# A two-part residual network kernel with fifteen own buffers for the first modulation's weights, and the pooled stage computed after its product

## The chip, the cores and the metric

The kernel runs on one core of a Trainium2 chip. The metric is device microseconds of one execution; before the change the three timed runs took 959.43, 956.2 and 955.88 us, median 956.2 us.

## The reference, cut to what matters

x is 256 tokens by 1024 features, all in fp32. The first of two stacks has two layers of two sublayers, each `x = x + gate * f(rms_norm(x) * (1 + scale) + shift)`. Shift, scale and gate come from one vector c: `silu(c) @ ada_w[layer, sub] + ada_b`, a 1024 x 3072 product for a single row, four times over (12 MB of weights each). f is, in turn: a hybrid of gated linear attention and sliding-window attention; an MLP (1024 to 4096, relu squared, back to 1024); the pooled mixer; and the same MLP with other weights. The second stack has an attention and retention mixer, a gated convolution MLP and an embedding gate.

The pooled mixer is the one that the change turns around:

```python
for gi, w in enumerate((2, 4, 8, 16)):          # 256 features per group
    csg = cs[..., lo:hi]                         # cumulative sums over tokens
    lag = jnp.pad(csg, ((0, 0), (w, 0), (0, 0)))[:, :S]
    pooled = (csg - lag) / cnt - hf[..., lo:hi]  # cnt = min(t + 1, w)
    outs.append(pooled.astype(h.dtype) @ pool_w[gi])
return jnp.concatenate(outs, axis=-1) * pool_scale
```

## The kernel before, in words

**Layout.** X lives in SBUF feature-major, eight tiles X[:, t, :] of 128 features by 256 tokens. Every fp32 operand of a large product is split into a high part rounded to fp32r and a low part, and a product is three fp32r matmuls (hi*hi, hi*lo, lo*hi: L557 to L559).

**Weight blocks.** All weights but the modulation's go through 135 numbered blocks of 1 MB (eight tiles of 128 x 256). Block n is loaded by SyncE into raw[n % 4] once w_lo of block n - 4 is made (L408), ScalarE makes w_hi (`split_hi`, L1786), VectorE makes w_lo (`split_lo`, L1123), and TensorE uses them (`block_used`). w_hi and w_lo have two buffers each, so the split of block n + 2 begins when block n is used. The order of work on each engine is written out by hand; each engine's program is one straight list with semaphores, so an instruction that waits holds everything behind it.

**Modulation.** The 96 pieces of ada_w (128 x 1024, 512 KB) are loaded by GpSimd, and VectorE multiplies each by one value of silu(c) per partition and adds it to an accumulator (`ada_sum`, L1142; first ones L1137). Pieces 0 to 7 are the first sublayer's scale, 8 to 15 its shift, 16 to 23 its gate. They go through three slots ada_raw, except `ADA_EARLY`, which have places of their own: six halves of the raw buffers and two attention tiles. The sum over the 128 partitions is then taken either by TensorE transposes into a PSUM bank and a VectorE reduction (`turn_sums` L660, `part` L1174), or by 1-column matmuls with ones (`add_sums`, L670; the second sublayer's gate and the third's three parts).

**Opening.** SyncE issues constants, c, x, thirteen small vectors, rel_bias, w_gla, sinks and the 16 glr columns; then `t8` (the relative bias table, a matmul L743) goes to DRAM (L435) and comes back skewed (`hankel`, tile MIX, L439, after 10 sums), and TensorE flips it (L758, four 128 x 512 fp32 products) between the scale's turn and the shift's turn (L660). Then `norm` (L1285), ScalarE's high part with the shift (L1808), VectorE's low part (L1268), and block 0.

**Attention.** The first sublayer's gate is turned between blocks 2 and 3. After the attention, ScalarE makes the mix's high part (L1813), then `split_hi(10)`; VectorE the low part (L1265), then `split_lo(10)`.

**MLP.** `up`: 16 blocks; VectorE fits 2, 1, 2, 1 sums of ada pieces into the four blocks of an iteration. `down`: four iterations of four blocks into PSUM A[0] and A[1], one iteration for two tiles of X; VectorE has 2, 2, 0, 0 sums after the splits, then `residual_tile` for both tiles (L1246, L1250, L1256), a split, and 2 more sums.

**Pooled stage.** After `down(0)`: scale sums (L670), the mean square of x (L649, root on ScalarE L1792, L1795), VectorE makes `factor(2)` and writes h without shift to pad[0] (L1560), waits for the shift sums (L670, `part` L1167), ScalarE adds the shift (L2030), VectorE runs 1 to 4 shifted additions per group (L1576), divides (L1583, L1584, L1587), ScalarE and VectorE split (L2035, L1265), and TensorE multiplies with block 45. The residual (L1215) needs the gate's sum. ScalarE squares X (L2040), TensorE sums (L941), and the last sublayer's norm (L1285, L1808, L1268) leads to `up(1)`.

## Time and profile before

| | |
|---|---|
| runs timed | 955.88, 956.2, 959.43 us; median 956.2 |
| profiled execution, its own time | 958.09 us |
| its span, first to last instruction | 956.4 us |
| TensorE busy, mean granted clock | 888.4 us (93%), 0.97 |
| VectorE busy | 692.1 us (72%) |
| ScalarE busy | 456.8 us (48%) |
| DMA | 196.60 MB, mean 206 GB/s |

### The profile page before, as it was taken

How to read it: one execution, taken by the hardware profiler on the slowest of the kernel's cores; microseconds unless marked ns; L12 is line 12 of the kernel's file. 1: busy time of each engine (PE TensorE's matmuls, PEld its weight loads, DVE VectorE, ACT ScalarE, POOL GpSimd, SP SyncE). 2: the span in 40 equal slices, each digit the busy share in tenths (PEclk: the TensorE clock that was granted, in tenths of full speed). 3: DMA queues.
4: the chain of work that ended last, by engine and by line, in shares of the span. 5: the costliest groups of instructions: out<-in, count | busy, mean ns of one | idle time of the engine just before them, and what ended most of it. 6: DMA issues, size and time to landing. Idle time of an engine off the chain costs nothing.

```text
span 956.4 us, 17671 instructions
## 1 busy us (share of the span) xinstructions
PE 888.4 (93%) x7028; PEld 852.6 (89%) x7028; DVE 692.1 (72%) x877; ACT 456.8 (48%) x573; POOL 58.0 (6%) x104
## 2 busy tenths in 40 slices
PE   2599999899999996799999999999999999999996
PEld 1388879799999996699999999988989999999996
DVE  4889878788878888766666556855487877776665
ACT  2347464566643333456663433444465444444445
POOL 2110110211111110000000000000000000000000
PEclk9789999999999996799999999999999999999998
DMA  9895755499989994057765555653435555654531
GB/s 336 300 339 193 244 200 177 130 319 322 317 306 330 330 316 134 23 184 234 239 199 176 175 183 168 197 166 130 157 90 177 177 179 187 218 173 158 169 126 44
DMA packets 156600, 196.60 MB, mean 206 GB/s; under 512 B 5341, under 2 KB 143116, under 8 KB 156556
## 3 DMA queue, kind: packets, MB, share of 16 engines
q1 hardware_dynamic: 142732, 145.64, 47.6%
q0 software_dynamic: 13824, 50.34, 14.4%
q8 instruction: 31, 0.51, 0.2%
q14 instruction: 13, 0.11, 0.0%
HBM read 194.90 MB, written 1.06 MB: 205 GB/s over the span
## 4 chain that ended last, share of the span: by engine, by line
PE 81%; DVE 9%; ACT 4%; issue 2%; DMA 2%; SPq 1%; DVEq 0%; ACTq 0%
PE G L557 15%; PE G L558 15%; PE G L559 15%; PE A L557 7%; PE A L559 7%; PE A L558 7%; DVE w_lo L1123 2%; ACT w_hi L1786 2%; PE G L632 2%; PE A L685 2%; PE G L633 2%; PE G L634 2%; DMA sinks<-in_attn_sinks_dram 1%; DMA MIX<-bias_rows 1%; DVE HN L1285 1%
## 5 line engine op out<-in xcount | busy, mean ns | idle before, releaser
L1123 DVE TENSOR_TENSOR w_lo<-raw,w_hi 128x2048 fp32r<-128x2048 f32 x135 | 307.1, 2275 | 163.7 <-ACT w_hi L1786 163.5
L1786 ACT ACTIVATE w_hi<-raw 128x2048 fp32r<-128x2048 f32 x135 | 256.6, 1901 | 265.7 <-PE A L559 132.4
L557 PE MATMUL G<-h_hi,w_hi 128*128 128x256 f32 x880 | 257.9, 293 | 22.5 <-DVE h_lo L1268 13.0
L558 PE MATMUL G<-h_lo,w_hi 128*128 128x256 f32 x880 | 253.3, 288 | 0.0
L559 PE MATMUL G<-h_hi,w_lo 128*128 128x256 f32 x880 | 253.2, 288 | 0.0
L557 PEld LDWEIGHTS G<-h_hi,w_hi 128*128 128x128 f32 x880 | 173.0, 197 | 29.5 <-issue 22.5
L558 PEld LDWEIGHTS G<-h_lo,w_hi 128*128 128x128 f32 x880 | 173.6, 197 | 0.2 <-issue 0.2
L559 PEld LDWEIGHTS G<-h_hi,w_lo 128*128 128x128 f32 x880 | 173.2, 197 | 0.0
L557 PE MATMUL A<-u_hi,w_hi 128*128 128x256 f32 x512 | 143.4, 280 | 0.7 <-DVE w_lo L1123 0.7
L558 PE MATMUL A<-u_lo,w_hi 128*128 128x256 f32 x512 | 142.9, 279 | 0.0
L559 PE MATMUL A<-u_hi,w_lo 128*128 128x256 f32 x512 | 142.9, 279 | 0.0
L557 PE MATMUL G<-e_hi,w_hi 128*128 128x256 f32 x368 | 104.2, 283 | 0.0
L558 PE MATMUL G<-e_lo,w_hi 128*128 128x256 f32 x368 | 104.2, 283 | 0.0
L559 PE MATMUL G<-e_hi,w_lo 128*128 128x256 f32 x368 | 104.1, 283 | 0.0
L557 PEld LDWEIGHTS A<-u_hi,w_hi 128*128 128x128 f32 x512 | 96.2, 188 | 1.3 <-DVE w_lo L1123 1.3
L558 PEld LDWEIGHTS A<-u_lo,w_hi 128*128 128x128 f32 x512 | 96.2, 188 | 0.0
L559 PEld LDWEIGHTS A<-u_hi,w_lo 128*128 128x128 f32 x512 | 96.2, 188 | 0.0
L557 PEld LDWEIGHTS G<-e_hi,w_hi 128*128 128x128 f32 x368 | 70.7, 192 | 0.0
L558 PEld LDWEIGHTS G<-e_lo,w_hi 128*128 128x128 f32 x368 | 70.7, 192 | 0.0
L559 PEld LDWEIGHTS G<-e_hi,w_lo 128*128 128x128 f32 x368 | 70.7, 192 | 0.0
L1142 DVE SCALAR_TENSOR_TENSOR ada_acc<-ada_raw,c_silu,ada_acc 128x1024 f32<-128x1024 f32 x52 | 65.7, 1280 | 4.7 <-DMA ada_raw<-in_ada_w_dram 3.7
L557 PE MATMUL A<-f_hi,w_hi 128*128 128x256 f32 x176 | 49.7, 282 | 1.8 <-DVE HN L1240 1.8
(325 smaller groups left out, 1315.7 us busy)
## 6 DMA issues: line engine op xcount, KB each, us to landing
raw<-in_mlp_w_dram SPq DMA_DIRECT2D x64, 1024.0 KB, 5.5
ada_raw<-in_ada_w_dram POOLq DMA_DIRECT2D x88, 512.0 KB, 5.7
raw<-in_w_in_dram SPq DMA_DIRECT2D x14, 1024.0 KB, 5.0
raw<-in_w_up_dram SPq DMA_DIRECT2D x11, 1024.0 KB, 5.4
raw<-in_w_gate_dram SPq DMA_DIRECT2D x11, 1024.0 KB, 5.3
raw<-in_attn_w_in_dram SPq DMA_DIRECT2D x9, 1024.0 KB, 7.1
raw<-in_w_down_dram SPq DMA_DIRECT2D x8, 1024.0 KB, 5.2
raw<-in_attn_w_out_dram SPq DMA_DIRECT2D x4, 1024.0 KB, 5.4
```

What stands on the lines that cost most here:

```text
L557: pe.matmul(dst, wh, ah, start=start, stop=False)
L558: pe.matmul(dst, wh, al, start=False, stop=False)
L559: return pe.matmul(dst, wl, ah, start=False, stop=stop)
L632: pe.matmul(dst, h_hi[:, t, toks], w_hi[n % 2][:, t, cols], start=t == 0, stop=False)
L633: pe.matmul(dst, h_hi[:, t, toks], w_lo[n % 2][:, t, cols], start=False, stop=False)
L634: last = pe.matmul(dst, h_lo[:, t, toks], w_hi[n % 2][:, t, cols], start=False, stop=t == KT - 1)
L685: last = pe.matmul(dst[:, e, 0:keys], Q4[half, hp, b * P:b * P + P], K4[half, kt, 0:keys], start=True, stop=True)
L1123: dve.tensor_tensor(w_lo[n % 2][:, 0:k, :], raw[n % RAW][:, 0:k, :], w_hi[n % 2][:, 0:k, :].bitcast(F32), ALU.subtract).then_inc(lo_done, 1)
L1142: dve.scalar_tensor_tensor(out=acc, in0=src, scalar=c_silu[:, bass.ds(i * 2 + k, 1)], in1=acc, op0=ALU.mult, op1=ALU.add).then_inc(ada_use ...
L1285: ins = dve.scalar_tensor_tensor(out=HN[p % 2][:, m, :], in0=X[:, t, :], scalar=gain[:, t:t + 1], in1=roots[:, :], op0=ALU.mult, op1=ALU.mult)
L1786: act.activation(w_hi[n % 2][:, 0:k, :], raw[n % RAW][:, 0:k, :], ACT.Copy).then_inc(hi_done, 1)
```

## The change

**Opening.** Pieces 3 to 15 and 19, 20 now have places of their own (five raw halves and ten tiles that the attention needs only later), so scale and shift are issued without waiting, but for piece 15, which waits for the table's way to DRAM; gate pieces wait for raw block 1. rel_bias is loaded third and its table is sent before x; x is issued behind the thirteen vectors. The skewed table is fetched before block 0, not after ten sums. The scale is summed along rows by ScalarE (`rows_along`, four copies in place with accumulator reads); VectorE norms the four pairs into HN0 with pieces 11 to 14 between them, then splits block 0, then adds piece 15; the shift's two halves are summed by ScalarE and VectorE, and only the two splits with the shift follow. The first gate is turned after the attention and summed by ScalarE before `split_hi(10)`.

**Pooled stage.** The product comes first: X times the gain, split like e_hi and e_lo inside `down(0)`, is multiplied with block 45 token-major; the result is scaled with the token's root and the shift's own product (sw, made by two ones matmuls from parts made in `down(0)`) is added, and the pooling is four 128 x 144 and 128 x 128 band matrices, applied by fp32 matmuls. VectorE makes the bands in `down(0)`. The sums of the second sublayer's gate and the third's scale and shift are turned between `up(0)` and `down(0)` in the G banks; up's sums stand as 2, 2, 2, 0; the last iteration of down has its last two before the residual. Three blocks of up(1) are loaded before SyncE waits for the sw parts.

```diff
-ADA_EARLY = (3, 4, 5, 6, 7, 8, 19, 20)
+ADA_EARLY = (*range(3, 16), 19, 20)
...
-                 for n in range(6)] + [b[:, :, :].rearrange("p t s -> p (t s)") for b in (GE, GG)]
+                 for n in range(5)]
+        early += [b[:, :, :].rearrange("p t s -> p (t s)") for b in (Q4, K4, V4, GV)] + [
+            PT[:, :, :, :].rearrange("p a b s -> p (a b s)"),
+            wide[:, 4:6, :].rearrange("p a b -> p (a b)"), wide[:, 6:8, :].rearrange("p a b -> p (a b)"),
+            SS[:, :, :, :].rearrange("p a b s -> p (a b s)")]
...
-                sp.dma_start(x_rows, x[0].rearrange("(k p) d -> p k d", p=P)).then_inc(x_in, 16)
+                sp.dma_start(rb[:, :], rel_bias).then_inc(rb_in, 16)
...
+                bank_was_read(sp, "table")
+                sp.dma_start(scratch.ap(), t8[:, :]).then_inc(table_out, 16)
+                sp.dma_start(x_rows, x[0].rearrange("(k p) d -> p k d", p=P)).then_inc(x_in, 16)
...
                 sp.wait_ge(table_out, 16)
-                sp.wait_ge(ada_used, 10)
                 sp.dma_start(hankel[:, :, :],
                              bass.AP(scratch, 0, [[1, P], [HANKEL, HEADS], [1, S]])).then_inc(table_in, 16)
+                load(N_ATTN, w_in[:, :, ATTN_COLS[0]:ATTN_COLS[0] + COLS])
+                sp.wait_ge(early_full[ADA_EARLY.index(2 * DT - 2)], 16)
                 for j, col in enumerate(ATTN_COLS[1:], 1):
                     if j < RAW:
-                        sp.wait_ge(ada_used, (14, 16, 16)[j - 1])
+                        sp.wait_ge(ada_used, (5, 7, 8)[j - 1])
...
+                if f == 2 * DT - 1:
+                    pool.wait_ge(table_out, 16)
+                if f == 2 * DT:
+                    pool.wait_ge(raw_full[1], 16)
...
-            def add_sums(m, name, blocks):
...
+            def turned_free(m, part, u, blocks):
                 pe.wait_ge(ada_used, blocks)
-                for t in range(DT):
-                    last = pe.matmul(dst[:, t:t + 1], sums_of(m, part)[:, part, t * P:(t + 1) * P],
-                                     ones[:, 0:1], start=True, stop=True)
-                bank_done(f"{name}{m}", last)
-            def scale_and_shift(m):
-                for name in ("scale", "shift"):
-                    turn_sums(m, name, {1: ADA_C, 3: ADA_E}[m])
+                for half in range(2):
+                    g_empty(u + half)
+                    for t in range(4):
+                        at = (4 * half + t) * P
+                        last = pe.transpose(G[(u + half) % 4][:, t * P:(t + 1) * P],
+                                            sums_of(m, part)[:, part, at:at + P], ident)
+                    last.then_inc(sums_turned, 1)
+            def token_sums(name, norm):
+                pe.wait_ge(ssq_ready, SQUARES[norm])
...
-            turn_sums(0, "gate", ADA_B)
...
+            turn_sums(0, "gate", ADA_B)
...
-            add_sums(1, "gate", ADA_D - 2)
+            for n, (m, part) in enumerate(((1, GATE), (2, SCALE), (2, SHIFT))):
+                turned_free(m, part, U_SUMS + 2 * n, ADA_D)
             down(0)
-            add_sums(2, "scale", ADA_D)
-            mean_square(2)
-            add_sums(2, "shift", ADA_D)
-            add_sums(2, "gate", ADA_E)
             block_ready(N_POOL)
+            def pool_group(g):
+                pe.wait_ge(e2_ready, 2 * g + 2)
+                for k in range(2):
+                    u = U_POOL + 2 * (g // 2) + k
+                    if g % 2 == 0:
+                        g_empty(u)
+                    dst = halves(G[u % 4])[:, g % 2, :]
+                    toks = slice(k * P, k * P + P)
+                    for t in (2 * g, 2 * g + 1):
+                        pe.matmul(dst, h_hi[:, t, toks], w_hi[N_POOL % 2][:, t, :], start=t == 2 * g, stop=False)
+                        pe.matmul(dst, h_hi[:, t, toks], w_lo[N_POOL % 2][:, t, :], start=False, stop=False)
+                        last = pe.matmul(dst, h_lo[:, t, toks], w_hi[N_POOL % 2][:, t, :], start=False,
+                                         stop=t % 2 == 1)
+                return last
+            pool_group(0)
+            pool_group(1).then_inc(pool_done, 1)
+            pool_group(2)
+            token_sums("ms2", 2)
+            pe.wait_ge(sw_ready, 1)
+            for p in range(2):
+                pe.wait_ge((down_free0, down_free1)[p], 5)
+                dst = bank_empty(pe, f"sw{p}")
+                bank_done(f"sw{p}", pe.matmul(halves(dst), ones[:, :], HN[p][:, :, :], start=True, stop=True))
+            turn_sums(2, "gate", ADA_E)
+            pool_group(3).then_inc(block_used, 1)
+            turn_sums(3, "scale", ADA_E)
             for g in range(4):
-                g_empty(U_POOL + g)
+                if g == 2:
+                    turn_sums(3, "shift", ADA_E)
+                for k in range(2):
+                    u = U_POOL + 2 * (g // 2) + k
+                    pe.wait_ge(g_free[u % 4], u // 4 + 1)
+                u = U_POOL + 4 + g
+                g_empty(u)
                 for m in range(2):
-                    if m == 0:
-                        pe.wait_ge(h_ready, 4 * SPLIT["pool"] + g + 1)
-                    last = feature_tile(N_POOL, halves(G[(U_POOL + g) % 4])[:, m, :], slice(m * P, m * P + P),
-                                        [(2 * g, 2 * g), (2 * g + 1, 2 * g + 1)], h_hi, h_lo)
-                last.then_inc(pool_done if g < 3 else block_used, 1)
-            scale_and_shift(3)
+                    dst = halves(G[u % 4])[:, m, :]
+                    cols = slice(g * COLS + m * P, g * COLS + m * P + P)
+                    pe.matmul(dst[:, 0:P + POOL_PAD], z_tok[:, 0, cols], band[:, g, :], start=True, stop=False,
+                              skip_group_check=True)
+                    last = pe.matmul(dst[:, P:S], z_tok[:, 1, cols], band2[g], start=False, stop=True,
+                                     skip_group_check=True)
+                last.then_inc(band_done, 1)
...
+            ada_next(6)
...
+            for p in range(4):
+                for t in (2 * p, 2 * p + 1):
+                    ins = dve.scalar_tensor_tensor(out=HN0[:, t, :], in0=X[:, t, :], scalar=GAIN[:, 0, t:t + 1],
+                                                   in1=rstd[:, :], op0=ALU.mult, op1=ALU.mult)
+                ins.then_inc(norm_ready, 1)
+                ada_next(1)
...
-                        for _ in range((2, 1, 2, 1)[j] if with_ada else 0):
+                        for _ in range((2, 2, 2, 0)[j] if with_ada else 0):
...
-                    part(1, "gate")
+                    for half in range(2):
+                        u = U_SUMS + half
+                        dve.wait_ge(sums_turned, half + 1)
+                        ins = dve.tensor_reduce(part_sums[:, 4 * half:4 * half + 4],
+                                                G[u % 4][:, :].rearrange("p (t k) -> p t k", t=4), AX_X, ALU.add)
+                        ins.then_inc(g_free[u % 4], 1)
+                        dve.wait_ge(g_free[u % 4], u // 4 + 1)
...
+                    for u in range(U_SUMS + 2, U_SUMS + 6):
+                        dve.wait_ge(g_free[u % 4], u // 4 + 1)
+                    chain(with_bias(6 * DT, 2 * DT, 0))
+                    chain(factor(2))
...
+                def band_of(g):
+                    v, head = C[:, C_DIST:C_DIST + P + POOL_PAD], band[:, g, 0:POOL_PAD]
+                    chain(dve.tensor_scalar(band[:, g, :], v, -float(P), 1.0 / (2 << g), ALU.is_ge, ALU.mult))
+                    chain(dve.scalar_tensor_tensor(out=band[:, g, :], in0=v, scalar=float((2 << g) - P),
+                                                   in1=band[:, g, :], op0=ALU.is_lt, op1=ALU.mult))
+                    chain(dve.tensor_tensor(band2[g], band[:, g, 0:P], ident, ALU.subtract))
+                    chain(dve.scalar_tensor_tensor(
+                        out=head, in0=v[:, 0:POOL_PAD], scalar=-float(P),
+                        in1=C[:, C_CNT_AT + g * POOL_PAD:C_CNT_AT + (g + 1) * POOL_PAD],
+                        op0=ALU.is_ge, op1=ALU.mult))
+                    chain(dve.scalar_tensor_tensor(out=head, in0=v[:, 0:POOL_PAD], scalar=float((2 << g) - P),
+                                                   in1=head, op0=ALU.is_lt, op1=ALU.mult))
+                    dve.tensor_tensor(band[:, g, 0:P], band[:, g, 0:P], ident, ALU.subtract)
+                def out_tiles(i, last, bands=()):
...
+                        if j == 2:
+                            for g in bands:
+                                band_of(g)
+                        if j == 2 and last:
+                            dve.wait_ge(sw_part, 1)
+                            for g in range(4):
+                                part = HN[g // 2][:, g % 2, :]
+                                at = 2 * g + 1
+                                ins = dve.scalar_tensor_tensor(out=part, in0=raw[N_POOL % RAW][:, at, :],
+                                                               scalar=MOD[:, 2, at:at + 1], in1=part,
+                                                               op0=ALU.mult, op1=ALU.add)
+                            ins.then_inc(sw_ready, 1)
+                        for _ in range((2, 2, 2 if last else 0, 0)[j] if with_ada else 0):
...
+                if layer == 0:
+                    for i, bands in enumerate(((0,), (1,), (2, 3), ())):
+                        out_tiles(i, i == 3, bands)
...
+            for p in range(2):
+                if p == 0:
+                    dve.wait_ge(pool_done, 1)
+                else:
+                    dve.wait_ge(block_used, N_POOL + 1)
+                bank_was_read(dve, f"sw{p}")
+                for k in range(2):
+                    u = U_POOL + 2 * p + k
+                    dve.scalar_tensor_tensor(out=z_tok[:, k, 512 * p:512 * p + 512], in0=G[u % 4][:, :],
+                                             scalar=t_rstd[:, k:k + 1], in1=sw[:, p, :], op0=ALU.mult,
+                                             op1=ALU.add).then_inc(g_free[u % 4], 1)
+            for half in "ab":
+                bank_was_read(dve, f"gate2{half}")
+            chain(with_bias(8 * DT, DT, 0))
             chain(dve.tensor_tensor(gate_ps[:, :], MOD[:, 2, 2 * DT:], V[:, V_PSCALE:V_PSCALE + DT], ALU.mult))
             for g in range(4):
...
+            def rows_along(bank, col):
+                for t in range(4):
+                    tile = bank[:, t * P:(t + 1) * P]
+                    ins = act.activation(tile, tile, ACT.Copy,
+                                         accum_out=mod_sums[:, col + t:col + t + 1])
+                return ins
...
+            for half in range(2):
+                src = bank_full(act, f"gate0{'ab'[half]}")
+                bank_read(f"gate0{'ab'[half]}", rows_along(src, 2 * DT + 4 * half))
             split_hi(10)
...
+            token_root("ms2", t_rstd)
+            for p in range(2):
+                src = bank_full(act, f"sw{p}")
+                bank_read(f"sw{p}", act.activation(sw[:, p, :], src[:, :], ACT.Copy))
+            for name, col in (("gate2", 0), ("scale3", 2 * DT), ("shift3", DT)):
+                for half in range(2):
+                    src = bank_full(act, f"{name}{'ab'[half]}")
+                    bank_read(f"{name}{'ab'[half]}", rows_along(src, col + 4 * half))
```

## Rows read from the trace of the kernel before

**Rows 1.** Windows over the span's stages

```profile
core 0: us, PE busy (x) PEld busy (x) DVE busy (x) ACT busy (x) POOL busy (x), PEclk, DMA share, GB/s
0.00:48.40 48.40, 17.88 (x62) 11.97 (x62) 30.91 (x45) 13.96 (x23) 11.34 (x25) 0.89 0.89 319
...
361.50:401.30 39.80, 25.46 (x135) 23.55 (x133) 32.69 (x72) 13.85 (x25) 1.42 (x2) 0.69 0.22 68
```

**Rows 2.** Windows of the opening, the same columns

```profile
12.00:20.00 8.00, 2.05 (x10) 1.43 (x8) 5.04 (x5) 2.06 (x4) 1.06 (x2) 1.00 1.03 384
...
28.00:36.00 8.00, 0.83 (x8) 0.59 (x6) 7.69 (x10) 2.69 (x3) 1.58 (x3) 0.76 0.81 263
```

**Rows 3.** DMA issues to 60 us: x, KB each, median us to landing

```profile
wide<-in_x_dram SPq DMA_DIRECT2D x1, 1024.0 KB, 9.6
MIX<-bias_rows SPq DMA_DIRECT2D x1, 1024.0 KB, 8.6
```

**Rows 4.** Timeline of all engines to 75 us: start, duration, what, idle before

```profile
18.89 0.71 PE L739 MATMUL A<-C,PR 128*128 128x128 f32 x3 [5.56 <-DMA PR<-in_conv_w_dram]
...
21.65 1.97 PE L729 MATMUL A<-C,wide 128*128 128x128 f32 x8
...
36.91 6.38 PE L758 MATMUL A<-MIX,C 128*128 128x512 f32 x8 [8.08 <-DMA MIX<-bias_rows]
...
48.44 0.36 PE L557 MATMUL G<-h_hi,w_hi 128*128 128x256 f32 x1 [4.27 <-DVE h_lo L1268]
```

**Rows 5.** Timeline of TensorE: end of block 0 (next product)

```profile
58.02 0.28 PE L557 MATMUL A<-h_hi,g_hi 128*16 128x256 f32 x1
```

**Rows 6.** Timeline of TensorE: turn of the first gate

```profile
76.23 1.04 PE L660 MATMUL A<-C,ada_acc 128*128 128x128 f32 x8
```

**Rows 7.** Groups by line: count, busy, mean ns (VectorE)

```profile
L1123 DVE TENSOR_TENSOR w_lo<-raw,w_hi 128x2048 fp32r<-128x2048 f32 x131 | 300.0, 2290 | 157.1 <-ACT w_hi L1786 156.9
L1142 DVE SCALAR_TENSOR_TENSOR ada_acc<-ada_raw,c_silu,ada_acc 128x1024 f32<-128x1024 f32 x52 | 65.7, 1280 | 4.7 <-DMA ada_raw<-in_ada_w_dram 3.7
...
L1174 DVE TENSOR_REDUCE part_sums<-A 128x4 f32<-128x512 f32 x16 | 11.0, 688 | 2.2 <-PE A L660 1.9
```

**Rows 8.** Groups by line: ScalarE's split, accumulator read, PSUM copy

```profile
L1786 ACT ACTIVATE w_hi<-raw 128x2048 fp32r<-128x2048 f32 x131 | 250.7, 1913 | 256.8 <-PE G L559 129.9 <-PE A L559 123.4 <-DMA raw<-in_attn_w_in_dram 2.5
...
L1841 ACT ACTIVATION_READ_ACCUMULATOR PR<-SS,stat 128x1 f32 x32 | 6.1, 189 | 0.0
...
L1848 ACT ACTIVATE MIX<-A 128x128 f32<-128x128 f32 x8 | 2.2, 272 | 1.2 <-PE A L707 1.2
```

**Rows 9.** VectorE: the low part of block 10

```profile
147.06 2.29 DVE L1123 TENSOR_TENSOR w_lo<-raw,w_hi 128x2048 fp32r<-128x2048 f32 x1 [1.11 <-ACT w_hi L1786]
```

**Rows 10.** TensorE between up(0) and down(0)

```profile
270.00 1.92 PE L670 MATMUL A<-ones,ada_acc 128*128 128x1 f32 x16
```

**Rows 11.** VectorE in the last block of up(0)

```profile
275.52 0.68 DVE L1513 TENSOR_TENSOR u_lo<-HN,u_hi 128x512 f32 x1
```

**Rows 12.** VectorE in down(0), third iteration: waits for ScalarE's split

```profile
324.43 2.29 DVE L1123 TENSOR_TENSOR w_lo<-raw,w_hi 128x2048 fp32r<-128x2048 f32 x1 [0.92 <-ACT w_hi L1786]
...
341.22 2.29 DVE L1123 TENSOR_TENSOR w_lo<-raw,w_hi 128x2048 fp32r<-128x2048 f32 x1 [0.39 <-ACT w_hi L1786]
```

**Rows 13.** TensorE around the pooled stage

```profile
361.47 1.84 PE L670 MATMUL A<-ones,ada_acc 128*128 128x1 f32 x16
...
395.33 1.89 PE L941 MATMUL A<-HN,ones 128*128 128x256 f32 x8
401.30 0.55 PE L557 MATMUL G<-h_hi,w_hi 128*128 128x256 f32 x1 [4.07 <-DVE h_lo L1268]
```

**Rows 14.** TensorE's granted clock around short stands (columns as rows 1)

```profile
139.00:145.00 6.00, 3.24 (x27) 2.27 (x25) 4.38 (x7) 4.20 (x10) 0.00 (x0) 1.00 0.02 9
...
366.00:390.00 24.00, 15.29 (x68) 14.70 (x69) 20.86 (x48) 6.49 (x13) 1.42 (x2) 0.51 0.14 45
401.00:408.00 7.00, 6.64 (x29) 6.09 (x30) 5.82 (x12) 3.62 (x5) 0.00 (x0) 0.53 0.01 2
```

302 lines of the change are left out of this document (160 added, 142 removed).

## The prediction

> **What bounds the kernel now.** I read the windows of the stages first [rows 1]. In the first 48.4 us TensorE is busy for 17.9 us, and in the 39.8 us from the end of `down(0)` to the first product of `up(1)` for 25.5 us at a mean clock of 0.69. In between it is nearly always busy, and there a change of another engine matters only if it makes TensorE wait. So the chain of waits was read in these two stretches, and the timelines of VectorE and ScalarE wherever the change gives them work beside TensorE.
>
> In the opening the reader is to see three things. The 16 DMA engines move 384 GB/s at first but only 263 GB/s at 28 to 36 us [rows 2]: pieces queue behind sums. VectorE and TensorE wait for the thirteen vectors, which are turned at 18.9 us. And the flips of the skewed table stand at 36.9 to 43.1 us, ahead of the shift's turn [rows 4]. Block 0 starts at 48.44 and ends at 58.0 [rows 4, 5].
>
> In the pooled stage VectorE is busy 32.7 of 39.8 us [rows 1], and TensorE stands at the lower clock, 0.51 from 366 to 390 us [rows 14].
>
> **Part 1, the opening.** Scale and shift are 16 pieces of 0.52 MB; with x, the table, block 0's weights and constants about 12 MB, at 384 GB/s [rows 2] 31 us. DMA ends near 33 us, so VectorE's list decides. x is now issued at about 9.5 us; with its 9.6 us of before [rows 3] it lands at 19 (bounds: 14, if it was the queue ahead of it that was slow, and 27, if the whole backlog goes first). Four turns, and ScalarE's square and copy of each pair, 1.1 us, end at 24; mean square, scale turn (eight transposes took 1.97 us on a TensorE that had stood [rows 4], 1.04 on a running one [rows 6]) and root at 26. `rows_along` is a PSUM copy and an accumulator read, 272 and 189 ns [rows 8], some 0.3 us with overlap: eight are 2.4 us, GAIN at 28.4. VectorE has by then done eleven sums; the vectors, no longer behind x, should reach it at about 15. Then four pairs of HN0 (0.85 each) with four sums at 1.2 (1280 ns, overlapped [rows 7]): 36.6; split of block 0 2.2 [rows 7] and g_lo: 39.1; last sum 40.3; turn at the lower clock 42.2; reduction 0.69 [rows 7] and two small sums 43.1; high part 44.1, low part 45.0. Block 0 starts 3.4 us earlier. Pairs then come every 0.9 us instead of every 1.65, and block 0, half of it at the lower clock, ends at 53.7: **-4.3 us**. Between -8 (x at 14) and +1 (x at 27, less what shorter waits at the end return).
>
> **Part 2, the first gate.** Its turn among the attention's products goes: -1.0 us [rows 6]. On ScalarE eight copies now stand before `split_hi(10)`. Before, the low part of block 10 waited 1.1 us for ScalarE and ended at 149.3 [rows 9], just before TensorE needed it. Plus 2.4 us it ends at 151.7; with some 0.6 us of lead TensorE waits 1.8. VectorE's two reductions are gone, in cover. Together **+0.8** (0 to +2).
>
> **Part 3, between up(0) and down(0).** Before, this seam cost TensorE 1.8 us [rows 10]. Now 24 transposes go into G banks, and the bank of the fifth turn is the first one's, that of the sixth the second's. They come free only by VectorE's reductions, which stand behind its last u_lo. That began at 275.5 after a sum of 1.2 us that is no longer there [rows 11]; so it ends at about 275.1, the reductions at 275.8 and 276.5, and the turns at 277.0. `down(0)` starts 5.2 us later than at 271.8 [rows 10]. ScalarE's own sixteen copies end at 278.6, before its next split is due. In these 7 us TensorE does 3 us of transposes. After a stand of 4.07 us [rows 13] it ran at 0.53 over 401 to 408 us [rows 14], 3 us lost; in 139 to 145 us, half busy, it kept 1.00 [rows 14]. I take 1.0. **+6.2** (+3 to +9).
>
> Here a rule speaks against the change. The trace shows the stretch of 139 to 145 us, which holds products and turns mixed, at the full clock [rows 14]. The Trainium skill ("TensorE: Matmul & The Clock Gate", Part 4: PE-mode transpose) says that transposes do not count as busy for the clock. By it this seam and the turns in the pooled stage would fall to 1.2 GHz; no row isolates this. It is the fourth case below.
>
> **Part 4, down(0).** VectorE gets 0.95 us of low parts per iteration and the bands. Two rows give it about 0.27 us plus 1 ns an element (1280 ns at 1024, 2290 at 2048 [rows 7]); with overlap 0.3 for 144 elements, 0.2 for 16: 1.6 us a band. What VectorE has over is 0.92 us at most blocks and 0.39 after the residual [rows 12], and of a block's 5.6 us ScalarE's split (1.9 [rows 8]) and VectorE's (2.3 [rows 7]), which begin when the buffer is free, leave some 1.3 us of lead. One band: 1.6 + 0.95 - 0.6 - 1.3 = 0.65 us of wait at the first block of the next iteration and 0.4 at its second, twice; two bands: 2.25 and 0.4. **+4.7** (+1, if the leads add up, to +7). The up loop's 2, 2, 2, 0 is hidden: its one-sum blocks had more over than a sum costs.
>
> **Part 5, the pooled stage**, counted from the end of `down(0)`. In the last iteration VectorE still has the split of block 45, the sw parts (1.9) and two sums (2.4) when TensorE is through: squares are ready at +5.5, e2's last low part at +6.5, the split of 46 at +9.3. TensorE: groups 0 to 2, 36 products at 0.117 us (16 blocks of 48 took the 89.6 us from 271.9 to 361.5 [rows 10, 13]): +4.2; waits for the squares +5.5; token sums +6.0; sw +7.9 (a 256-column fp32 product is 0.47 us [rows 13], 512 columns twice that); gate turn +8.9; group 3 +10.3; scale turn +11.3; bands 0, 1 +13.1; shift turn +14.1; bands 2, 3 +15.9. VectorE's z are ready before them; the residual ends at +16.9. ScalarE has 24 accumulating copies, 0.3 each, and comes to the squares of X late: +18.4. Sum +19.0, and from there root, norm and split as before, 4.1 us (397.2 to 401.3 [rows 13]): +23.05, against 39.8 [rows 1]. **-16.8** (-20 to -9, the latter if TensorE stays at the lower clock for half of it).
>
> Blocks from `up(1)` on are as before: the three blocks loaded early, and SyncE's wait for sw_ready behind them, are 15 us ahead of use. GpSimd's waits for the table and for raw block 1 hold only the gate's pieces, wanted after 50 us.
>
> **Sum**: -4.3 + 0.8 + 6.2 + 4.7 - 16.8 = -9.4 us. The profiled execution took 958.09 us for a span of 956.4 and would take 948.7; the median of the runs, 956.2, lies 1.9 below it, so the median after is 946.8, say **947**.
>
> **Rivals.**
> 1. The forecast, 942 to 951: 0.46.
> 2. The leads hold: VectorE's lateness in `down(0)` is absorbed (part 4 near +1, and squares then 2 us earlier), x lands early. For it: VectorE waited for ScalarE's splits before [rows 12], so there is time to catch up. Against: its new work stands in lumps. 956.2 - 9.4 - 5.7 = 941: 0.20.
> 3. The opening returns nothing: x lands at 27 us behind the thirteen pieces, and everything from the scale's root shifts. For it: in the first 20 us the engines are full [rows 2]. Against: x had its landing within 9.6 us with nine pieces queued [rows 3]. +4.3: 951: 0.14.
> 4. The lower clock holds at the seam (+2) and through half the pooled stage's turns and bands (+6): 955: 0.13.
> 5. Slower: the same mechanism through the whole stage. The seam costs 3 us more and its transposes 2; of the work from +6.0 to +15.9 all 9.9 us double, and the last sums and the opening's turns add 1.5: +16, 963 us. It decides from the point where TensorE is at 0.5 for over 14 us of work that I priced at full speed. For it: 24 us at 0.51 in this very place before [rows 14]. Against: TensorE comes to it from 90 us at the full clock and stands only 1.3 us. 0.07.
>
> **How the numbers follow.** A measurement of this kernel tells 0.5%, 4.8 us, from no change; the bound is 951.4. Faster: cases 1 and 2 and nearly half of 3: 0.72. Same: the rest of 3, case 4: 0.21. Slower: case 5: 0.07. The range leaves out case 5 and the tail of case 2 and takes in the others: 939 to 955.5. The cases of both signs are not close, so it is one range.
>
> **What would show it.** In the changed profile: first product of block 0 near 45 us, with the last sum's turn just ahead; one TensorE wait before block 10; a gap of 6 to 7 us between the last product of `up(0)` and the first of `down(0)` with two VectorE reductions in it; waits for w_lo in the iterations after the bands; 23 us from `down(0)` to `up(1)`, at a clock near 1. The prediction is wrong in part 1 if x lands before 15 or after 25 us, in part 3 if the clock after the seam is 0.5 for a block, in part 4 if the waits for w_lo are under 2 us, and as a whole if these stages balance.

## The result, and the profile after

The changed kernel takes 966.75 us (median of 4 runs, 964.47 to 967.42) against 957.57 us (4 runs, 955.88 to 959.43) for the kernel before: ratio 1.009, 95% interval 1.0066 to 1.0114. It is slower by 0.9%; I had said 947 and faster. The profiled execution took 964.47 us for a span of 962.8, so the forecast of -9.4 us stands against +6.4 between the two traces. The medians lie 9.2 us apart: the traced execution was 2.3 us under its kernel's median, that of the kernel before 0.5 above. The ledger below explains the 6.4.

Windows of the changed kernel over its stages, the columns of [rows 1]:

```profile
core 0: us, PE busy (x) PEld busy (x) DVE busy (x) ACT busy (x) POOL busy (x), PEclk, DMA share, GB/s
0.00:52.06 52.06, 17.43 (x63) 11.71 (x63) 30.63 (x47) 17.69 (x49) 11.38 (x25) 0.85 1.00 360
52.06:60.10 8.04, 8.04 (x49) 8.02 (x50) 7.00 (x10) 3.03 (x5) 0.00 (x0) 0.70 0.30 89
...
274.70:281.50 6.80, 3.15 (x26) 2.57 (x25) 6.09 (x7) 6.34 (x23) 1.05 (x2) 1.00 1.01 348
281.50:382.00 100.50, 93.92 (x771) 92.90 (x770) 77.49 (x90) 35.01 (x39) 11.08 (x21) 0.98 0.77 264
382.00:406.70 24.70, 18.77 (x133) 16.63 (x132) 17.79 (x36) 15.90 (x65) 1.42 (x2) 0.97 0.36 110
406.70:962.80 556.10, 543.75 (x4416) 530.33 (x4416) 369.51 (x470) 269.39 (x303) 3.69 (x7) 0.99 0.52 168
```

TensorE sets the end in every stage, so the first and last products of the stages make a ledger that closes:

| stage | before | after | measured | forecast |
|---|---|---|---|---|
| start to end of block 0 (part 1) | 58.02 | 60.03 | +2.0 | -4.3 |
| from there to up(0) (part 2) | 117.34 | 119.93 | +2.6 | +0.8 |
| up(0) | 94.56 | 94.61 | 0.0 | 0 |
| seam (part 3) | 1.86 | 6.90 | +5.0 | +6.2 |
| down(0) (part 4) | 89.70 | 100.46 | +10.8 | +4.7 |
| pooled stage (part 5) | 39.82 | 24.81 | -15.0 | -16.8 |
| up(1) to the end | 555.1 | 556.1 | +1.0 | 0 |
| sum | 956.4 | 962.8 | +6.4 | -9.4 |

The turned pooled stage gives its 15 us, at a granted clock of 0.97 against 0.69 [rows 1]. Four other stages spend more than that. Two rows of the table hold most of the miss: the opening (6.3 us) and down(0) (6.1 us).

**The opening.** The timeline of the changed kernel, all engines. x turns at 19.99 and the norm is multiplied from 30.49 on, about as forecast. But then:

```profile
34.64 6.29 PE L798 MATMUL A<-MIX,C 128*128 128x512 f32 x8 [7.00 <-DMA MIX<-bias_rows]
...
41.46 1.90 ACT L1912 ACTIVATE w_hi<-raw 128x2048 fp32r<-128x2048 f32 x1
...
43.39 2.29 DVE L1194 TENSOR_TENSOR w_lo<-raw,w_hi 128x2048 fp32r<-128x2048 f32 x1 [4.86 <-ACT w_hi L1912]
...
45.80 1.28 DVE L1213 SCALAR_TENSOR_TENSOR ada_acc<-SS,c_silu,ada_acc 128x1024 f32<-128x1024 f32 x1
...
47.22 1.94 PE L695 MATMUL A<-C,ada_acc 128*128 128x128 f32 x8 [6.30 <-DVE ada_acc L1213]
...
52.06 0.55 PE L592 MATMUL G<-h_hi,w_hi 128*128 128x256 f32 x1 [2.90 <-DVE h_lo L1339]
```

Read it from below: the first product waits for the shift, the shift's turn for the sixteenth sum, that sum stands behind block 0's low part, the low part behind its high part, the high part on ScalarE behind the four copies of the flips, and the flips wait for the skewed table. The table's row among the DMA issues says how late it was (8.6 us before [rows 3]):

```profile
wide<-in_x_dram SPq DMA_DIRECT2D x1, 1024.0 KB, 10.8
MIX<-bias_rows SPq DMA_DIRECT2D x1, 1024.0 KB, 19.8
```

**down(0).** Who TensorE waits for from 281.5 to 388 us:

```profile
PE A L592 <- DVE X L1317: 6.1, 3, 3.0
PE A L716 <- DVE sq_sum L1327: 1.2, 1, 1.2
PE A L592 <- DVE w_lo L1194: 0.4, 2, 0.2
```

and VectorE, in the same stretch:

```profile
DVE w_lo L1194 <- ACT w_hi L1912: 11.3, 8, 5.5
DVE late_acc L1213 <- DMA ada_raw<-in_ada_w_dram: 8.5, 7, 2.7
```

I had expected TensorE to wait for low parts. It waits 0.4 us for those and 6.1 us for `X`: the residual that reads banks A[0] and A[1] and so frees them. There is one pair of them, so the next output pair can't begin before. The worst of the three, as both engines show it:

```profile
350.65 1.28 DVE L1213 SCALAR_TENSOR_TENSOR late_acc<-ada_raw,c_silu,late_acc 128x1024 f32<-128x1024 f32 x1 [1.57 <-DMA ada_raw<-in_ada_w_dram]
351.86 2.28 DVE L1194 TENSOR_TENSOR w_lo<-raw,w_hi 128x2048 fp32r<-128x2048 f32 x1
354.06 0.23 DVE L1634 TENSOR_SCALAR band<-C 128x144 f32<-128x144 f32 x1
...
357.17 0.48 DVE L1317 SCALAR_TENSOR_TENSOR X<-A,MOD,X 128x256 f32<-128x256 f32 x1
...
357.70 0.58 PE L592 MATMUL A<-u_hi,w_hi 128*128 128x256 f32 x1 [3.04 <-DVE X L1317]
```

A sum that waits 1.57 us for its piece, a split, two bands (3.1 us) and only then the residual. Behind this stand TensorE's products come 0.21 us apart instead of 0.12 until 360.8: 1.4 us more. The products before and after it come at another pace than before the change too; that is the last group of experiments.

### The profile page after: what moved, and what is told of

The parts are those of the page before. It is cut to its first block, busy times and chain, and to the rows that moved or that the text cites. A ratio compares the mean times of both kernels' runs of the same rounds, so it can differ in the third digit from the quotient of the medians.

```text
span 962.8 us, 17732 instructions
## 1 busy us (share of the span) xinstructions
PE 888.2 (92%) x7036; PEld 850.9 (88%) x7036; DVE 682.9 (71%) x872; ACT 472.8 (49%) x695; POOL 58.0 (6%) x104
## 4 chain that ended last, share of the span: by engine, by line
PE 75%; DVE 10%; ACT 5%; DMA 5%; issue 3%; SPq 1%; ACTq 0%; DVEq 0%; POOLq 0%
PE G L592 14%; PE G L593 14%; PE G L594 14%; PE A L592 6%; PE A L594 6%; PE A L593 6%; DVE w_lo L1194 3%; ACT w_hi L1912 2%; DMA ada_raw<-in_ada_w_dram 2%; DMA MIX<-bias_rows 2%; PE G L667 2%; PE G L668 2%; PE G L669 2%; PE A L727 2%; DVE late_acc L1213 1%
## 5 line engine op out<-in xcount | busy, mean ns | idle before, releaser
L592 PE MATMUL G<-h_hi,w_hi 128*128 128x256 f32 x864 | 250.8, 290 | 15.2 <-DVE h_lo L1339 11.2
L593 PE MATMUL G<-h_lo,w_hi 128*128 128x256 f32 x864 | 246.8, 286 | 0.0
L594 PE MATMUL G<-h_hi,w_lo 128*128 128x256 f32 x864 | 246.6, 285 | 0.0
L592 PEld LDWEIGHTS G<-h_hi,w_hi 128*128 128x128 f32 x864 | 167.9, 194 | 21.2 <-issue 14.3
L593 PEld LDWEIGHTS G<-h_lo,w_hi 128*128 128x128 f32 x864 | 168.3, 195 | 0.2 <-issue 0.2
L594 PEld LDWEIGHTS G<-h_hi,w_lo 128*128 128x128 f32 x864 | 168.1, 195 | 0.0
L592 PE MATMUL A<-u_hi,w_hi 128*128 128x256 f32 x512 | 145.8, 285 | 6.6 <-DVE X L1317 6.1
L1213 DVE SCALAR_TENSOR_TENSOR ada_acc<-ada_raw,c_silu,ada_acc 128x1024 f32<-128x1024 f32 x45 | 57.1, 1280 | 5.4 <-DMA ada_raw<-in_ada_w_dram 4.9
```

The lines of the kernel that those rows point to most:

```text
L592: pe.matmul(dst, wh, ah, start=start, stop=False)
L593: pe.matmul(dst, wh, al, start=False, stop=False)
L594: return pe.matmul(dst, wl, ah, start=False, stop=stop)
L1213: dve.scalar_tensor_tensor(out=acc, in0=src, scalar=c_silu[:, bass.ds(i * 2 + k, 1)], in1=acc, op0=ALU.mult, op1=ALU.add).then_inc(ada_use ...
```

## The experiments

Medians, and ratios to the kernel before on the same chip. The runs were made on several chips, so where two variants are compared closely the ratios and their intervals count, not the difference of the medians.

| run | base and edit | us | ratio (95%) |
|---|---|---|---|
| e1_split_first | after, opening's order | 963.22 | 1.0076 (1.0055 to 1.0097) |
| e2_hold | e1, seven pieces held for the table | 962.85 | 1.0055 (1.0026 to 1.0083) |
| e7_hold_x | e1, five pieces held for x | 961.05 | 1.0028 (1.0005 to 1.0050) |
| e10_opening2 | after, x early, shift's turn first | 962.72 | 1.0036 (1.0009 to 1.0062) |
| h1_opening_only | before, with after's opening | 963.75 | 1.0049 (1.0031 to 1.0067) |
| h3_opening_ordered | h1, with e1's order | 959.12 | 1.0001 (0.9990 to 1.0013) |
| e4_bands_seam | after, bands ahead of down(0) | 960.71 | 1.0030 (1.0019 to 1.0040) |
| e5_bands_after | after, bands behind the sums | 960.23 | 1.0030 (1.0017 to 1.0043) |
| e8_last | e4, residual first at the end | 956.96 | 0.9999 (0.9986 to 1.0011) |
| e3_seam_gate | after, six banks; block 10 first | 961.33 | 1.0039 (1.0026 to 1.0053) |
| c2_all | all of it | 949.85 | 0.9905 (0.9869 to 0.9942) |
| c3_all | e10's opening, bands 3 + 1 | 947.15 | 0.9875 (0.9848 to 0.9902) |
| c4_all | c3 with e1's opening | 946.06 | 0.9852 (0.9826 to 0.9877) |
| p1_spare96 | before, one unused tile | 960.88 | 1.0028 (1.0013 to 1.0043) |
| p2_mod256 | c4, u and f moved back | 944.49 | 0.9850 (0.9830 to 0.9870) |
| p3_h32 | p2, h moved by 32 bytes | 938.63 | 0.9795 (0.9772 to 0.9817) |
| p5_e32 | p3, e moved too | 933.83 | 0.9756 (0.9734 to 0.9778) |
| p4_before_h32 | before, h moved by 32 bytes | 952.62 | 0.9945 (0.9925 to 0.9966) |

### The opening

**e1_split_first.**

```diff
@@ ScalarE
+            split_hi(0)
             for q in range(4):
                 src = bank_full(act, f"flip{q}")
...
-            split_hi(0)
@@ VectorE
+            ada_next(1)
             split_lo(0)
...
-            ada_next(1)
```

> The changed kernel with two moves in the opening and nothing else: ScalarE splits block 0 ahead of the four copies of the flips, and VectorE does the sixteenth sum ahead of block 0's low part. Theory (order): the changed kernel's block 0 starts at 52.06 us because the high part (41.5 to 43.4) stood behind copies that wait for the skewed table, and the last sum and the shift's turn stood behind the low part. Block 0's weights are in by about 37.6 us, so high part to 39.5, low part to 42, sum by 40, turn 41 to 43 behind the last flip, first product at 46.5: 5.5 us earlier, about 961 against 966.75. Rival (the loads decide): block 0's own weights or the piece land so late that the order is worth under 1.5 us, about 966.

The timeline of this kernel, the same places as above:

```profile
35.90 1.91 ACT L1912 ACTIVATE w_hi<-raw 128x2048 fp32r<-128x2048 f32 x1 [5.07 <-DMA raw<-in_attn_w_in_dram]
...
37.59 1.28 DVE L1213 SCALAR_TENSOR_TENSOR ada_acc<-SS,c_silu,ada_acc 128x1024 f32<-128x1024 f32 x1
...
44.04 0.36 PE L592 MATMUL G<-h_hi,w_hi 128*128 128x256 f32 x1 [3.61 <-DVE h_lo L1339]
```

The first product stands 8.0 us earlier than in the trace of the changed kernel, and no load was issued otherwise. But not all of the 8.0 is order: the table landed at 32.8 us here and at 34.6 there. In the six traces with the changed kernel's opening (after, e3, e4, e5, e8, h1) the first product stands at 49.8 to 52.1, in the six with this order (e1, h3, c4, p2, p3, p5) at 44.0 to 45.5, so order is worth about 6 us. The theory holds for the place. In the medians 3.5 us are left, and the intervals of the two ratios overlap. Part of that is block 0's clock: in this trace it ran at full speed, 6.0 us long, in the eight others with the two moves (e2, e7, h3, c2, c4, p2, p3, p5) partly or mostly at the lower clock, 7.0 to 8.5; and the traced execution (958.13) was by 4.4 us the fastest of the five. In it down(0), with its stops, took 103.5 us, 3.1 more than in the changed kernel.

**e2_hold** and **e7_hold_x.**

```diff
@@ GpSimd, e2
-                if f == 2 * DT - 1:
-                    pool.wait_ge(table_out, 16)
+                if f == 9:
+                    pool.wait_ge(table_in, 16)
@@ GpSimd, e7 (on e1)
+                if f == DT + 3:
+                    pool.wait_ge(x_in, 16)
```

> As the run before, and GpSimd issues the seven last pieces of the shift only when the skewed table has landed. Theory (bytes ahead): the table took 19.8 us from issue (14.8) to landing (34.6) because the engines, at about 400 GB/s, had some 7.7 MB queued; with 3.7 MB of it held back it lands within 11 us, by 26, and the flips end by 33; the held pieces come from 26 on at 1.3 us each, so the first product stands between 43 and 46, 1 to 3 us ahead of the run before. Rival (the queue's own packets): the table waits for the 64-byte rows of the gate's weights ahead of it on SyncE's queue, whatever GpSimd issues; then it still lands at 30 or later, the held pieces come only then, and the first product is 5 us or more later than in the run before.

The DMA issues of e2, and VectorE's first sum behind the hold:

```profile
MIX<-bias_rows SPq DMA_DIRECT2D x1, 1024.0 KB, 9.8
...
28.49 1.28 DVE L1212 SCALAR_TENSOR_TENSOR ada_acc<-K,c_silu,ada_acc 128x1024 f32<-128x1024 f32 x1 [6.67 <-DMA K<-in_ada_w_dram]
```

With 3.7 MB held back the table lands in 9.8 us instead of 19.1, with the 64-byte rows ahead of it on SyncE's queue as before (they took 11.0 us in place of 20.6): what it waited for was the bytes already queued. The engines are full all the time (1.00 in the window above), so it is a matter of whose bytes go first. The hold took as much from VectorE, which then waited 6.67 us: first product 46.15, 2.1 us behind e1 and not ahead of it as I had said, and the time is e1's.

> The kernel with the two moves in the opening, and GpSimd issues the five last pieces of the shift only when x has landed. Theory (bytes ahead, and what is late is x, not the pieces): x lands 2 to 3 us earlier (by 16.5), everything up to the factor with it, no sum waits more than 1 us for a held piece, and the first product stands at 41 to 42.5 instead of 44.0. Rival (the last pieces decide): the held pieces land late and VectorE waits for them over 2 us; first product 44 or later.

The theory fell. x still landed 10.0 us after its issue, as with all pieces queued (10.4); the pieces issued behind it had not delayed it. First product 45.08, 1.0 us behind e1's, and yet the ratio is the lower one (1.0028 against 1.0076): what the first product gains and what the kernel gains don't go together here.

**e10_opening2.**

```diff
@@ SyncE
                 sp.dma_start(rb[:, :], rel_bias).then_inc(rb_in, 16)
+                sp.dma_start(x_rows, x[0].rearrange("(k p) d -> p k d", p=P)).then_inc(x_in, 16)
...
@@ TensorE
+            turn_sums(0, "shift", 2 * DT)
             pe.wait_ge(table_in, 16)
             for q in range(4):
...
-            turn_sums(0, "shift", 2 * DT)
```

ScalarE copies the flips behind block 1's split, and VectorE does g_lo behind block 0's low parts.

> The changed kernel with its opening put in order of what lands first: x issued ahead of the thirteen vectors; the shift's turn ahead of the flips; the flips' copies and the gate's low part behind block 0's high and low parts. Theory (what is late is x by its place in the queue, then block 0's own weights): x lands by 13 us in place of 20, the factor stands at 25 to 26 in place of 30.3, the last sum ends at 34, and block 0's split (weights in at 36 to 37.6) decides: first product at 41 to 42 instead of 52.06. Rival (one bandwidth): bytes that x takes early are missing for the pieces, the sums of the scale end later and the factor gains under 2 us; first product at 44 or later. Either way a part of it may be lost behind: the kernel at 957 to 961 against 966.75.

46.92, so the rival. x took 10.2 us again and was in by 13, but now the vectors came at 18.5 and TensorE turns them ahead of x; the factor stood at 29.75 as ever (30.29 in the changed kernel). The kernel at 962.72 missed the 957 to 961 that I had given for either case. Of vectors and x, the one that SyncE issued last came at 18 to 20 us in every one of these openings.

**h1_opening_only** puts the changed opening, as it is, on the kernel before; **h3_opening_ordered** adds e1's two moves.

> The kernel before with the opening of the changed one alone (fifteen own buffers, the table's and x's new places in SyncE's order, the norm multiplied ahead of the shift, the accumulating copies, the flips ahead of block 0's split); the first gate, the seam, down(0) and the pooled stage are those of before. Theory (stage by stage): block 0 starts 3.6 us and ends 2.1 us later, and nothing behind it changes: 959.5 to 960.5 against 957.5 for before. Rival (the opening gains and something behind it loses): block 0 earlier than 48.4 us, and the kernel at or under 957.

> The kernel before with the changed opening alone and in it the two moves of order: the first part of the change as it was meant. Theory: the part as I priced it is right but for the order; block 0 starts at 44 to 45 in place of 50.5 with the unordered opening, everything behind it follows, and the kernel takes 956 to 958 against 963.75 for the unordered one, 1 to 3 us ahead of the kernel before. Rival (half of it comes back): as in the changed kernel, where 8.0 us at block 0 in the trace were 3.5 in the medians, the loads of blocks 1 to 10 or the clock take half back: 960 or more.

h1 measured 963.75 against 959.03, 4.7 us slower where the ledger of its stages in the opening says 0.6 at the end of block 0 (58.58). h3 was 4.6 us faster than h1, so here the 5.6 us at block 0 stay. But it only equals the kernel before, although it ends block 0 at 53.02, 5.0 us ahead of it. From there its stages are longer than those of before, by 0.9, 0.4, 1.5, 1.3 and 2.5 us, and so are h1's, to 0.2 us. Something that comes with the opening makes the later stages longer. The last group finds most of it.

### down(0) and the pooled stage

**e4_bands_seam** and **e5_bands_after.**

```diff
@@ e4, VectorE ahead of down(0)
                     chain(factor(2))
+                    for g in (0, 1, 2, 3):
+                        band_of(g)
...
@@ e5, VectorE in out_tiles
-                        if j == 2:
-                            for g in bands:
-                                band_of(g)
...
                     for _ in range(6 - done if with_ada else 0):
                         ada_pair(1, done, i)
                         done += 1
+                    for g in bands:
+                        band_of(g)
```

> The changed kernel with the four bands computed in one go before down(0), where VectorE stood idle for 5.5 us, and none inside it. Theory (one bank pair): the residual at the end of each output pair frees the only two accumulators, so whatever stands ahead of it on VectorE stops TensorE at once, and each stop makes VectorE take its pieces in a lump and wait for their loads (8.5 us of such waits against 3.4 before): with the bands gone the stops and most of the load waits go too, down(0) takes 90 to 92 us instead of 100.5, and the kernel comes to about 957.5. Rival (the loads are late by themselves): the load waits stay near 8.5 us and down(0) takes 95 or more, about 961 to 963.

> The changed kernel with each iteration's bands moved from ahead of its residual to behind its last two sums: the same work in the same iteration. Theory (place): down(0) takes 90 to 93 us, about 958. Rival (amount): VectorE has 21.2 of each 22.4 us to do wherever the bands stand, and with the load waits it doesn't fit; down(0) stays above 96 us, 962 to 966.

e4: down(0) took 92.65 us, with a stop of 0.6 us for a residual and one of 0.2 for a low part. The stops are the bands'. But load waits of VectorE didn't go, 10.1 us, so the rival's half is right too. Its lateness showed at the end instead; e4's pooled stage, windows and TensorE's wait in it:

```profile
373.84:403.38 29.54, 22.45 (x135) 19.01 (x133) 19.37 (x39) 16.18 (x65) 1.42 (x2) 0.85 0.32 99
...
380.85 1.83 PE L716 MATMUL A<-ones,sq_sum 128*128 128x1 f32 x8 [2.04 <-DVE sq_sum L1327]
```

Eight one-column products took 1.83 us where they take 1.05 at full speed: after standing, TensorE came back at the lower clock (0.85 over the stage). So 7.8 us won in down(0) were 3.1 at up(1), and 6.0 in the medians. e5: down(0) 96.1 us, between the two; its wait was of the kind that I had forecast, 1.6 us for a low part. Inside down(0) the place of the bands is worth 4.3 us and their absence another 3.5; but the two kernels take the same time (both 1.0030), since e4 gives the difference back in the pooled stage (29.5 us against 27.0).

**e8_last.**

```diff
+                        if j == 1 and last:
+                            ada_pair(1, done, i)
+                            done += 1
-                        if j == 2 and last:
                             dve.wait_ge(sw_part, 1)
...
-                        for _ in range((2, 2, 2 if last else 0, 0)[j] if with_ada else 0):
+                        for _ in range((2, 1 if last else 2, 0, 0)[j] if with_ada else 0):
```

> The kernel with the bands ahead of down(0), and in the last output pair VectorE does the residual as soon as TensorE is through: the sw parts go up between two sums, where VectorE waited 2.3 us for a load, and the last two sums behind the second norm's low parts. Theory (order at the end): of the 29.5 us that this kernel's pooled stage took, 4.2 were sw parts and sums ahead of the residual while TensorE stood until its clock fell; it takes 24 to 25.5, and the kernel about 956.5 against 960.7. Rival (the loads keep VectorE late): whichever order, the last sums wait for their loads, the gate's turn follows them, and the stage stays at 28 or more.

The split of block 46 stands behind the last two sums here. 956.96, as said. The pooled stage:

```profile
374.90:398.60 23.70, 18.84 (x135) 16.78 (x133) 17.40 (x35) 16.02 (x65) 1.42 (x2) 1.00 0.39 123
```

5.8 us less with the same work, at a clock of 1.00 (down(0) took 2.4 us more than in e4, with load waits of 9.1 us).

### The first gate and the seam

**e3_seam_gate.**

```diff
@@ ScalarE
+            split_hi(10)
             for half in range(2):
                 src = bank_full(act, f"gate0{'ab'[half]}")
...
-            split_hi(10)
@@ TensorE, the seam (gate1a and gate1b take banks 3 and 2)
-            for n, (m, part) in enumerate(((1, GATE), (2, SCALE), (2, SHIFT))):
-                turned_free(m, part, U_SUMS + 2 * n, ADA_D)
+            turn_sums(1, "gate", ADA_D - 2)
+            for n, (m, part) in enumerate(((2, SCALE), (2, SHIFT))):
+                turned_free(m, part, U_SUMS + 2 * n, ADA_D - 1 + n)
```

> The changed kernel with two edits in stretches that don't touch: ScalarE splits block 10 ahead of the first gate's eight accumulating copies; and the turns of the second layer's first gate go to two banks that down(0) leaves free, so that six banks take the six turns and none waits for a reduction. Theory (each wait is what stands ahead of it in its queue): TensorE's 1.76 us before block 10 goes to under 0.3, and the seam between up(0) and down(0) shrinks from 6.9 us to 3.4 (24 transposes at 0.13 us and the start), together -5 us, about 961.5. Rival 1: the gate's copies, now later, hold the residual and the wait moves to block 11 or 12, no gain there. Rival 2: the seam's turns still wait for VectorE's last sum and last low part, and the seam stays above 5 us.

The changed kernel's wait in the seam, for the bank of the fifth turn:

```profile
280.42 1.29 PE L706 MATMUL G<-C,ada_acc 128*128 128x128 f32 x8 [2.48 <-DVE part_sums L1615]
```

In e3 both edits did what was forecast: no wait ahead of block 10, and the seam 3.14 us. The banks are not all of it: the gate's turn no longer waits for the last two sums either (ADA_D - 2), where TensorE had stood 1.16 us at the start of the seam. The timeline of e3's:

```profile
272.23 1.04 PE L695 MATMUL A<-C,ada_acc 128*128 128x128 f32 x8
273.11 1.47 PE L706 MATMUL G<-C,ada_acc 128*128 128x128 f32 x12
...
275.37 0.36 PE L592 MATMUL A<-u_hi,w_hi 128*128 128x256 f32 x1
```

The medians are 5.4 us lower, but not by these two stages alone: in the trace down(0) and the pooled stage gave 3.5 us back and block 0 ended 2.5 us earlier, in an opening that is the changed kernel's. The stretch before up(0) kept 1.2 us of its 2.6: VectorE has three sums ahead of the tiles that the turn into bank `kend` reads (L1502) where it had one, and TensorE waits 1.5 us there.

### All together

c2 joins e7, e3, e4's and e8's edits, and in the first three output pairs both engines split ahead of the second norm's parts:

```diff
@@ ScalarE
+                        if j == 3 and not layer and not last:
+                            split_hi(N_DOWN[layer] + j + 2, i)
                         if j == 3:
...
@@ VectorE
+                    if not layer and not last:
+                        split_lo(n + 2, i)
                     gain, hi, lo = (gain5, e_hi, e_lo) if layer else (GAIN[:, 2, :], h_hi, h_lo)
```

> All edits together: opening as in the run before, block 10 split ahead of the gate's copies, six banks at the seam, bands ahead of down(0), the last output pair in the new order, and in the first three pairs the split ahead of the second norm's parts on ScalarE and VectorE. By the theory of queue order the stages add up: opening -10, gate -1.8, seam -3.5, down(0) and pooled stage 125.3 to about 117, so -8: about 943.5, 14 us faster than the kernel before the change. Rival (the loads give it back): with each stage earlier the pieces and weights aren't there, down(0) stays above 96 us, and the kernel comes out at 948 to 953.

949.85: between the two. One wait was new, at the second block of down(0), and what it costs is twice its length, since the 6.3 us behind it (my next expectation says 6.7) ran at the lower clock, 2.9 us more:

```profile
288.27 0.58 PE L594 MATMUL A<-u_hi,w_hi 128*128 128x256 f32 x1 [2.96 <-DVE w_lo L1197]
```

With the seam short, four bands (6.2 us) no longer fit ahead of the split.

c3 has e10's opening and this split of the bands:

```diff
@@ VectorE ahead of down(0), before the banks' wait
-                    for g in (0, 1, 2, 3):
+                    for g in (0, 1, 2):
                         band_of(g)
@@ VectorE in the first output pair
+                        if j == 1:
+                            for g in bands:
+                                band_of(g)
```

> The combination with that opening, and the bands split three ahead of the banks' wait before down(0) and one inside its first output pair (in the combination before, four of them made TensorE wait 3.0 us for a low part and run 6.7 us at the lower clock behind it). Theory: first product at 41 to 42, seam 3.1, down(0) 91 to 93 in place of 97.2, pooled stage 23.5: about 940 to 943. Rival (loads): the earlier opening finds blocks 1 to 3 not landed and down(0) stays at 96 or more: 948 or more.

> The last combination with the first repair of the opening in place of the second: only block 0's split ahead of the flips' copies and the last sum ahead of its low part, x and the shift's turn where the change has them. Theory: what is behind the opening keeps what it measured in the last combination (seam 3.1, down(0) 91.8, pooled stage 23.5), and block 0 starts at 44 instead of 48.06: 942.5 to 944.5 against 947.15. Rival (the clock takes it): block 0 then runs at the lower clock, as in two of three kernels with this opening, and ends within 1.5 us of 54.0: 946 to 948.

c3: down(0) 91.8 as said, but block 0 at 48.06. c4: block 0 at 44.97, mostly at the lower clock, ending at 53.23; 946.06, the rival's number for the rival's reason.

### Where the tiles lie

```diff
@@ p1_spare96, on before
         part_sums = sb("part_sums", [P, DT])
+        spare = sb("spare", [P, 3 * DT])
@@ p2_mod256, on c4
-        mod_sums = sb("mod_sums", [P, 3 * DT])
+        mod_sums = sb("mod_sums", [P, 64])
@@ p3_h32, on p2 (mod_sums 56)
+        spare = sb("spare", [P, 8])
         h_hi = sb("h_hi", [P, DT, S], F32R)
```

> The kernel before and nothing of the change but one unused tile of 96 bytes a partition, where the change puts its new tile of accumulated sums: it moves every tile behind it by 96 bytes, u_hi, u_lo, f_hi and f_lo among them. Theory (address): TensorE's products over those tiles come every 116.7 ns in the trace of before and every 118.7 ns in all ten traces of kernels with the new tile, while products over h_hi, which lies ahead of it, come every 120.0 in all; so the unused tile alone brings 118.7 ns in down(0), down(1) and the last down stretch, 2 ns by 768, 768 and some 530 products, 4 us: 961 to 962.5 against 958 for before. Rival (the change's own traffic or chance of the run slows them): the pitch stays 116.7 and the time is that of before within 1 us.

down(0), in the window of before and in that of p1, busy without a gap in both:

```profile
271.78:361.48 89.70, 89.70 (x771) 89.70 (x771) 73.73 (x61) 30.87 (x19) 12.05 (x23) 1.00 0.93 322
```

```profile
270.77:361.99 91.22, 91.22 (x770) 91.22 (x770) 74.40 (x62) 30.83 (x19) 12.10 (x23) 1.00 0.91 317
```

The same 768 products by the same instructions take 1.5 us more because of an empty tile of 96 bytes: 116.7 to 118.7 ns. In the medians 2.7 us where I had said 4. Against before, the later stages of p1 are longer by 0.1, 0.0, 1.5, 0.8 and 2.1 us, 4.5 of the 6.6 of h3; the other 2.1 us, 1.3 of them in the attention and up(0), stay unexplained.

> The last combination with the tile of accumulated sums stretched from 96 to 256 bytes a partition, so that u and f lie at the same place within 256 bytes as in the kernel before; not one instruction differs. Theory (address): pitch 116.7 ns in the three stretches again and 4 us less, about 942 against 946.06. Rival: no change, 945 to 947.

The pitch went back to 116.7 ns, and down(0) was still 92.4 us: with faster products TensorE waited 2.2 us for residuals where it had not waited. The stages behind it are 1.8 us shorter, block 0 ended 0.6 later. The ratio, 0.9850 against 0.9852, shows no difference. The rival has the time, the theory the pitch.

> As the run before, and h_hi and h_lo moved by 32 bytes too (an unused tile of 32 bytes ahead of them, the sums' tile 32 bytes shorter, so that u and f stay). Theory (what matters is the place of the moving tile against the weights' tiles): h's products go from 120.0 to about 116.7 ns, 3.3 ns on some 4,000 products, 10 to 13 us less: 930 to 933. Rival (only whole or half 64 bytes of u's own rows, or u's own stretches): h's pitch stays 120.0 and the time equals the run before within 1 us.

> As the run before, with the unused 32 bytes ahead of e_hi instead of ahead of h_hi, so that e_hi and e_lo (120.0 ns a product from about 690 to 820 us in the run before) stand 32 bytes off the weights' place too. Theory (distance from the weights' tiles within 256 bytes): their products come every 116.7 to 117 ns as well, some 1,000 products by 3.2 ns, 3 us less where TensorE is the bound: 935 to 936.5 against 938.63. Rival (VectorE and ScalarE are by now the bound in these blocks): the pitch falls and waits take its place, 938 to 939.

> The kernel before, with h_hi and h_lo moved by 32 bytes and u and f kept at their place within 256 bytes, and nothing else. Theory (address alone): its h products go from 120.0 to 117 ns, and as in the combination (5.9 us) it gains 5 to 7 us: 951 to 953; the combination's orders are then worth 13 to 15 us on either base. Rival: TensorE is less often the bound in this kernel, gain under 3 us.

p3: h's products at 117.0 ns in up(0), 5.9 us less in the medians, half of what I said, since TensorE then waits more. p5: e's at 116.7, 933.83. p4: h's at 117.8, and 32 unused bytes (with 224 more behind, to keep u in place) make the kernel before 4.4 us faster, a little under the 5 to 7 that I had given. The 32 bytes move every tile between h and the next unused one, and in p5 X too; that h's and e's products speed up is what the pitch shows.

| moving tile less weights' tile, modulo 256 bytes | ns a product |
|---|---|
| 0 (h and e in before and after) | 120.0 |
| 128 (u, f in after, p1) | 118.7; up to 120.0 in stretches of others |
| 32 (u, f in before, p2, p3; h in p3, p4, p5; e in p5) | 116.7 to 117.8 |

The Trainium skill ("TensorE: Matmul & The Clock Gate", Part 2, Step-by-step: what each phase is for) says that the weights' load has a read port of its own and takes nothing from the running matmul. Something in these rows depends on the distance or on the moving tile's own address; both fit the three places, and I have no run that parts them. If it is the distance, the rows don't agree with the page; if it is the address alone, they say nothing of it.

Nor is the place the whole story. In down(0) of e5, with the changed kernel's addresses, the products come 120.0 ns apart from 330 us on, at a clock of 1.00, and so in stretches of e1, e3, e7 and c4 (119.0 to 120.0):

```profile
330.00:360.00 30.00, 29.92 (x249) 29.70 (x248) 26.70 (x32) 11.14 (x8) 4.22 (x8) 1.00 0.84 289
```

And h's products come at 117.8 in p4 and mostly at 116.7 in p3, from the same addresses. What makes this difference is open.

## Why the prediction was wrong, step by step

The forecast was 15.8 us off, and two steps hold 12.4 of it: in part 1 that VectorE's list decides the opening, in part 4 that the bands delay low parts. In both the work and its durations were about right, and what it stands in front of was not.

**Part 1, wrong in sign.** x, root, factor and the norm's pairs came within 2 us of what I said. The step that failed is "DMA ends near 33 us, so VectorE's list decides". The first half was nearly right (the table landed at 34.6, block 0's weights at 35.9 in e1) and speaks against the second: what VectorE has in its list ("split of block 0 2.2 [rows 7] and g_lo: 39.1; last sum 40.3") waits for ScalarE, which does four copies of the flips first, and these wait for the load that lands last. I priced the split and the last sum by duration and never followed the table's 8.6 us [rows 3] behind the bytes of fifteen issued pieces and x. Order alone is worth about 6 us at the first product (5.6 between h1 and h3; 8.0 in e1's trace, of which the earlier table is 1.8). My bounds went to +1; the trace shows +2.0. The size is that of one pair of traces: block 0 ends at 57.3 to 60.0 in six traces of the new opening and at 56.5 to 58.0 in three of the old one (before, p1, p4), +1.4 on the average.

**Part 2.** The wait before block 10 was 1.76 us against 1.8 forecast, and e3 removed it. The rest of the +2.6 is `kend`.

**Part 3, right.** +5.0 against +6.2: the first down product at 281.47, 6.9 us after up(0), at the full clock. The microsecond for the clock was not needed.

**Part 4, right in kind of work, wrong in what it holds.** A band took 1.55 us, as estimated (1.6), but I let it delay low parts, whose 1.3 us of lead absorb it, and forgot that it stands ahead of the only instruction that frees A[0] and A[1], which has no lead at all. By the starts of its products, down(0) has six gaps that take 7.7 us above the pace (6.1 for residuals, 0.4 for low parts, the rest to get going again), 1.4 us of lower clock and 1.5 us of slower pace: 10.6 of the 10.8 us.

**Part 5, right.** 24.8 us against 23.05. Cases 4 and 5 fell: the clock was 0.97 in the stage and 1.00 in the seam, with 48 transposes in them. By the rule that I weighed (the Trainium skill, "TensorE: Matmul & The Clock Gate", Part 4: PE-mode transpose) it should have fallen; these traces show nothing of it: the seam holds transposes alone, 24 of them, with 3.6 us of standing, and the products behind it come at the full clock; in the pooled stage they are mixed with products.

**What no step had.** "Blocks from up(1) on are as before": they are, in instructions, and take 1.0 us longer. By the pitch it should be some 4 us with down(0)'s 1.5; the empty tile alone gave 2.7 in the medians (p1), with 2.9 us behind down(0) in its trace, so something there gives the changed kernel about 2 us back, and what it is I don't know. It is a cost of the change that is in no engine's list: a declaration moved the operands.

By the ledger these are 6.3 + 1.8 + 6.1 + 1.8 + 1.0 - 1.2 = 15.8 us, the distance from -9.4 to +6.4. What stays open: the ledger closes for the traces only, 6.4 us, and the medians say 9.2. And e1's trace ends block 0 10.0 us earlier and the kernel 6.3, as down(0) takes 3.1 more and up(0) with the seam 0.9, while its median is 3.5 lower; of this the clock of block 0 explains some 2.4, and the early table of the one trace against the late one of the other 1.8.

## What to carry to other kernels

When work is moved to before a point, look for what each queue holds ahead of the one instruction that others have no buffer for (a residual that frees the only accumulators, a split behind copies of something that is not urgent), and price the load that lands last by the bytes queued ahead of it, not by its old duration. After any change of declarations compare the distance between successive products in a stretch that it didn't touch: 32 bytes in front of a tile were worth 4.4 us here, and the turned stage and the opening with the orders put right gave 946.06 us, 1.5% under the kernel before (c4). With the tiles moved as well it is 933.83 us, 2.4% under; the last step is not a gain of the change, since the kernel before gains by moved tiles too.

## What the runs showed of the hardware that I had not expected

- TensorE's pace on 128x256 fp32r products depends on where the moving tile lies: 120.0, 118.7 and 116.7 ns for 0, 128 and 32 bytes off the weights' tile modulo 256 in most stretches of twenty traces. An empty tile alone changes it (p1: 116.7 to 118.7, clock 1.00 in both windows). At 128 it was 119.0 to 120.0 in parts of e1, e3, e5, e7 and c4, at 32 it was 117.8 in p4.
- x, 1 MB, landed 9.6 to 10.8 us after its issue in nineteen of the twenty traces (12.0 in c2), whether it was issued at 1.7 us or at 10 and whatever was held back behind it; the table went from 19.1 to 9.8 us when 3.7 MB ahead of it were held.
- A stand of 3 us costs TensorE another 1.4 us here (clock 0.51 behind it) and 2.9 in c2 (0.50) by the lower clock; one of 2.5 us (331.13) cost none (1.00), while one of 2.0 us in e4's pooled stage was followed by the lower clock. The length of the stand alone doesn't tell it.
